# Three pieces brought together: the first stage written as one, an earlier place for the second block's residual, and another unit order in the first output product

## The reference, cut to what matters

```python
def first_block(...):
    mod = jnp.split((jax.nn.silu(c) @ w_ada[l] + b_ada[l])[:, None, :], N_MOD, axis=-1)
    ...
    h_lat = _modulate(_rmsnorm(x, norm1_g[l]), sh1, sc1)
    h_ctx = _modulate(_rmsnorm(ctx, norm1_g[l]), sh1c, sc1c)
    mix_l, mix_c = _token_mixer(h_lat, h_ctx, ...)     # begins with h @ w_in, ends with y @ w_out
    x = x + g1 * mix_l
    x = x + g2 * _swiglu(_modulate(_rmsnorm(x, norm2_g[l]), sh2, sc2), w_ffn_in[l], w_ffn_out[l])
    return _rmsnorm(x, final_norm_g)

def second_block(...):
    ...                                                # mixer: recurrence, banded attention, gates
    x = x + merged @ w_out[l]
    xn2 = rmsnorm(x, norm_ffn_g[l])
    gu = xn2 @ w_ffn_in[l]
    ff_gate, ff_up = jnp.split(gu, [D_FF_2], axis=-1)
    x = x + (jax.nn.silu(ff_gate) * ff_up) @ w_ffn_out[l]
    return rmsnorm(x, norm_final_g)
```

## Time and profile before

| what | us |
|---|---|
| median of 3 runs | 3408.72 |
| lowest, highest | 3406.57, 3416.22 |
| the profiled execution's own time | 3411.13 |
| its span | 3409.8 |
| PE busy in it | 3261.6 (96%) |
| DVE, ACT, POOL busy | 1928.6, 1379.7, 384.0 |
| mean granted TensorE clock | 0.984 |

### The profile page before, as it was taken

One profiled execution on the slowest core, in us unless ns is written; L12 is line 12 of the kernel. 1 busy time (PEld: TensorE's weight loads), 2 busy tenths in 40 slices (PEclk: granted clock), 3 DMA queues, 4 the chain that ended last, 5 costly groups with the idle time before them and its releaser, 6 DMA issues. The chain is left out here.

```text
span 3409.8 us, 39604 instructions
## 1 busy us (share of the span) xinstructions
PE 3261.6 (96%) x14862; PEld 2651.7 (78%) x14862; DVE 1928.6 (57%) x3098; ACT 1379.7 (40%) x2325; POOL 384.0 (11%) x605
## 2 busy tenths in 40 slices
PE   6999999999999999999999999998888799999998
PEld 3888888878888778888888888877556588888886
DVE  4474433456334387777445454664676587777443
ACT  4593222244333243333233355554575343333221
POOL 0121100002100300000011101111211200001011
PEclk8999999999999999999999999999999899999999
DMA  5366444346543323334852434445744523335752
GB/s 220 107 206 197 134 126 135 124 148 224 190 156 99 126 90 118 105 118 150 254 176 81 164 108 148 134 147 164 163 93 105 185 90 121 112 111 170 240 182 75
DMA packets 228045, 494.14 MB, mean 145 GB/s; under 512 B 21520, under 2 KB 84624, under 8 KB 226320
## 3 DMA queue, kind: packets, MB, share of 16 engines
q1 hardware_dynamic: 147728, 302.30, 28.0%
q0 software_dynamic: 80128, 189.30, 17.0%
HBM read 353.63 MB, written 137.89 MB: 144 GB/s over the span
## 5 line engine op out<-in xcount | busy, mean ns | idle before, releaser
L290 PE MATMUL p<-s_xh,s_wh 128*128 128x512 f32 x2256 | 901.6, 400 | 32.9 <-DVE s_tmp L401 12.3
L291 PE MATMUL p<-s_xl,s_wh 128*128 128x512 f32 x2256 | 885.3, 392 | 0.0
L292 PE MATMUL p<-s_xh,s_wl 128*128 128x512 f32 x2256 | 885.2, 392 | 0.0
L290 PEld LDWEIGHTS p<-s_xh,s_wh 128*128 128x128 f32 x2256 | 428.6, 190 | 127.3 <-issue 22.6
L292 PEld LDWEIGHTS p<-s_xh,s_wl 128*128 128x128 f32 x2256 | 427.5, 190 | 91.2
L291 PEld LDWEIGHTS p<-s_xl,s_wh 128*128 128x128 f32 x2256 | 428.4, 190 | 88.8 <-issue 1.7
L2126 PE MATMUL p<-s_xh,s_wh 128*128 128x512 f32 x1152 | 449.5, 390 | 2.1 <-DVE s_xl L2233 1.1
L2128 PE MATMUL p<-s_xh,s_wl 128*128 128x512 f32 x1152 | 448.2, 389 | 0.0
L2127 PE MATMUL p<-s_xl,s_wh 128*128 128x512 f32 x1152 | 448.2, 389 | 0.0
L250 DVE TENSOR_TENSOR s_wl<-s_ws,s_wh 128x1024 fp32r<-128x1024 f32 x157 | 195.3, 1256 | 232.9 <-ACT s_wh L242 232.6
L2126 PEld LDWEIGHTS p<-s_xh,s_wh 128*128 128x128 f32 x1152 | 216.3, 188 | 48.8 <-issue 4.2
(11 more groups left out here) (381 smaller groups left out, 5102.4 us busy)
## 6 DMA issues: line engine op xcount, KB each, us to landing
d_h<-s_fhl POOLq DMA_DIRECT2D x80, 512.0 KB, 3.2
s_ws<-i_Wf SPq DMA_DIRECT2D x48, 512.0 KB, 4.3
s_qb<-i_Wf SPq DMA_DIRECT2D x40, 512.0 KB, 4.0
s_qb<-i_Wf SPq DMA_DIRECT2D x80, 256.0 KB, 3.1
s_ws<-i_Wf SPq DMA_DIRECT2D x80, 256.0 KB, 2.9
s_aw<-i_adaT SPq DMA_DIRECT2D x32, 512.0 KB, 3.6
s_xh<-d_h POOLq DMA_DIRECT2D x16, 1024.0 KB, 12.1
s_xl<-d_h POOLq DMA_DIRECT2D x16, 1024.0 KB, 14.8
```

Of the source, the lines that this page charges most:

```text
L290: pe.matmul(o, wh, H[:, k, c:c + n], start=(k == 0), stop=False)
L291: pe.matmul(o, wh, L[:, k, c:c + n], start=False, stop=False)
L292: last = pe.matmul(o, wl, H[:, k, c:c + n], start=False, stop=(k == 7))
```

## The change

**First stage.** `stage0` now holds the context's, half 0's and half 1's work up to the first three groups. SP issues w_ada first, loads the four first weight tiles between them (two into ACC and RB, since WS has two slots), and takes x as half tiles, half 0 ahead of half 1. The weights are split while w_ada is multiplied. The squares have memory of their own; those of half 1 are made between the context's high parts and added on POOL. The spreading of half 0 stands inside the context's group, sums and spreading of half 1 inside half 0's group. The context's keys go to DRAM from ACC.

```diff
+            for k in range(8):
+                sp.dma_start(AD[:, k, :], D["ada"][k]).then_inc(*ad_in[k].up())
...
+                elif 2 <= k < 6:
+                    weights_sp(k - 1)
+                elif k == 6:
+                    x_sp(0, range(4))
+            x_sp(0, range(4, 8))
+            x_sp(1, range(8))
...
+            products_pe(firsts[0], {3: lambda: spread_pe(0)})
+            products_pe(firsts[1], {1: lambda: columns_pe(1), 3: lambda: spread_pe(1)})
+            products_pe(firsts[2])
...
+            for k in range(8):
+                high_act("c", k)
+                if k < 6:
+                    square_act(1, 2 + k)
+            for k in range(2):
+                high_act(0, k)
+            ACW.wait_ge(*w_lo.at(3))
+            for g, p in enumerate(firsts[0][1:]):
+                ACW.wait_ge(*p.mm)
+                ac.activation(ACC[:, 256 * g:256 * g + 256], B[p.bank][:, 0:256], ACT.Copy).then_inc(*evA.up())
+            al_act(0)
+            root_act(1)
+            for k in range(2, 8):
+                high_act(0, k)
```

```diff
+        pairs = plan_pairs(name, [(0, 0), (0, 1), (1, 0), (1, 1), (2, 0), (3, 0), (2, 1), (3, 1)])
...
+                products_pe(js, {5: lambda: sums_pe(s0)} if (p, h) == (2, 1) else {0: lambda: spread_pe(0, DIA[:, 0, :], s0.diag, n0.q[7])} if (p, h) == (3, 1) else None)
...
+                    norm_dve(n0, scale, shift, {1: lambda: after_dve(js), 4: lambda: weights_dve(ahead(pairs[7][2][0].i, 2))})
...
-                products_pe(e.js, {3: lambda: sums_pe(s1), 6: lambda: spread_pe(1, DIA[:, 1, :], s1.diag, q1[7])} if e is plain[0] else None)
+                products_pe(e.js, {0: lambda: sums_pe(s1), 3: lambda: spread_pe(1, DIA[:, 1, :], s1.diag, q1[7])} if e is plain[1] else None)
```

```diff
+        items += [("wo2", m, "new first", "kept", (PART[:, m, :], sc_mm.at(128)), "wo2", 1.0, TC) for m in range(4, 8)]
...
         def sp_():
+            SPW.wait_ge(*attended.scores)
+            for m in range(8):
+                residual_sp(m, 0)
+                if m < 4:
+                    for t in written[("wo2", m)]:
+                        SPW.wait_ge(*t)
+                    sp.dma_start(PART[:, m, :], dW2[m][:, 0:512]).then_inc(*part_in[m].up())
             weights_sp(ahead(pairs[0][0].i, 2) + NS)
...
+            for m in range(8):
+                SPW.wait_ge(*summed.at(m + 1))
+                residual_sp(m, 1)
...
-            products_pe(pairs[1], {6: lambda: sums_pe(s0)})
-            products_pe(pairs[2], {4: lambda: spread_pe(0, DIA[:, 0, :], s0.diag, n0.q[7])})
+            products_pe(pairs[1])
+            products_pe(pairs[2], {2: lambda: sums_pe(s0), 6: lambda: spread_pe(0, DIA[:, 0, :], s0.diag, n0.q[7])})
```

More of the change, by code:

```diff
@@ L471, in stage0 @@
         which = {"c": 0, 0: 1, 1: 2}
[L473 to L492, removed]
@@ L507, in squares_dve @@
-        def squares_dve(j):
-            what, k = sums[j]
-            if k:
-                q = slots.index(j)
-                DVW.wait_ge(*squares.at(j + 1))
-                DVW.wait_ge(*added.now())
-                dv.tensor_tensor(total[what], total[what], TMP[:, q % NT, 0:size[what]], ALU.add).then_inc(*added.up())
-        def modulated_act(what):
-            s, c, H, L, c0 = dst[what]
-            n = size[what]
-            for k in range(8):
-                q = which[what] * 8 + k
-                ACW.wait_ge(*shifted.at(q + 1))
-                ac.activation(H[:, k, c0:c0 + n], TMP[:, q % NT, 0:n], ACT.Identity, bias=shift_of[what][:, k:k + 1]).then_inc(*x_hi.up())
@@ L555, in stage0 @@
-        spread_bank = {"c": 7, 0: 4, 1: 5}
+        column_bank, spread_bank = {"c": 6, 0: 6, 1: 3}, {"c": 4, 0: 5, 1: 3}
         scale_of = {"c": GS[:, 8:16], 0: GS[:, 0:8], 1: GS[:, 0:8]}
         shift_of = {"c": MODC, 0: MOD, 1: MOD}
-        def spread_pe(what, free):
-            n = size[what]
-            PEW.wait_ge(*diag.at(which[what] + 1))
-            for t in free:
-                PEW.wait_ge(*t)
-            pe.matmul(B[spread_bank[what]][:, 0:n], ones[:], DIA[what], start=True, stop=True).then_inc(*spread.up())
@@ new lines, in ada_pe, with columns_pe @@
+        def ada_pe(k):
+            PEW.wait_ge(*silu.at(1))
+            PEW.wait_ge(*ad_in[k].at(1))
+            for c in range(4):
+                last = pe.matmul(B[c][0:2, :], sc2[:, k, :], AD[:, k, c * 512:c * 512 + 512], start=(k == 0), stop=(k == 7))
+            last.then_inc(*ada.up())
+        def columns_pe(what):
+            PEW.wait_ge(*{"c": added.at(7), 0: added.at(14), 1: added1.at(7)}[what])
+            PEW.wait_ge(*const.at(1))
+            if what == 1:
+                PEW.wait_ge(*spread3_free)
+            for j in range(size[what] // 128):
+                c = 4 * which[what] + j
+                last = pe.matmul(B[column_bank[what]][:, c:c + 1], SQ[what][0][:, 128 * j:128 * j + 128], ones[:, 0:1], start=True, stop=True)
+            last.then_inc(*colsum.up())
@@ new lines, in al_dve, with square_dve @@
+        def al_dve(part):
+            p = firsts[part][0]
+            lo = AL[32:64, p.col:p.col + p.n]
+            DVW.wait_ge(*al_hi.at(part + 1))
+            dv.tensor_tensor(lo, B[p.bank][32:64, 0:p.n], lo.bitcast(F), ALU.subtract).then_inc(*al_lo.up())
+        def square_dve(what, k):
+            n = 8 * which[what] + k
+            DVW.wait_ge(*squares.at(n + 1))
+            DVW.wait_ge(*added.now())
+            dv.tensor_tensor(SQ[what][0], SQ[what][0], SQ[what][k], ALU.add).then_inc(*added.up())
@@ L765, in pe_ @@
         def pe_():
-            for part, group in enumerate(firsts):
-                products_pe(group)
             for what, j in steps:
@@ L3328, in stage7 @@
             f = Plan()
[L3329 to L3330 removed]
+            f.m, f.done = m, summed.due()
             ready[(m, 0)] = f.done
```

598 lines of the change are left out of this document (301 added, 297 removed).

## The result

| | before | after |
|---|---|---|
| median, us (lowest to highest) | 3407.6 (3404.8 to 3416.2) | 3372.9 (3371.9 to 3373.9) |
| profiled execution, us | 3411.1 | 3372.0 |
| its span, us | 3409.8 | 3370.7 |
| PE busy, us | 3261.6 | 3253.0 |

The ratio of after to before is 0.9894, 95% interval 0.9876 to 0.9912. The change takes 34.7 us off the median. The forecast was 3365 with a range of 3352 to 3382: sign and range held. The question for the experiments is which term of the sum was too big.

What follows compares the result with a forecast made beforehand. PE, busy 3261.6 of 3409.8 us, was taken as the bound, leaving its waits and half-clock matmuls to win. Gains 22 + 3.6 + 18.4 = 44.0 off the median 3408.7 gave 3364.7, say 3365 us; range 3352 to 3382.

Steps and rivals of the forecast that it cites:

- A: First stage: half 1's group ends at 104.3 instead of 126.8 us; gain taken as 22 us, bounds 10 and 24.
- Rival 1: First stage gains only half, 11 us, because data slip or ACT or POOL is late: 3376 us; chance 0.16.
- The port beside the context's modulation: Context's group: DVE and POOL exclude each other, up to 10 us on DVE, hidden by PE's pace but for 0.5.
- B: First output product: half 1's spreading 5.0 us earlier, less 1.4 for restart, gains 3.6 us; bounds 0 and 7.
- C: Second output product: gain 19.8 us from earlier loads and covered waits, less 1.4 for restart, 18.4; bounds 12 and 20.
- Rival 2: Second output product meets a new wait, SP's weights behind eight loads or ACT's squares; C 10, 3373 us; chance 0.11.
- The cover that goes: Both blocks, at P1: less PE work follows half 1's spreading, so PE waits 8.2 and 6.9 us; restart costs 1.9.
- Rival 3: P1 does not wait because DVE's list up to it shortens: 3347 us; chance 0.06.
- Rival 4: Granted clock stays low after the two new idles at P1, making it slower, 3425 us with 60 per block; chance 0.02.
- Rival 5: The change does not do what it says, loads and sums fall where they fell: 3409 us; chance 0.03.

Runs made afterwards that it cites:

- a_only: The kernel before with only the first stage of the change, everything else old; 3387.6 us, ratio 0.9941 to before.
- weights_before_x: The change, but in the second output product SP issues the fourth pair's weights between the fourth and fifth of eight x loads; 3367.5 us.
- best: The change plus weights between x loads, half 1's spreading in first plain pair, its root before weights, last residual inside first output product's norm; 3352.2 us.
- two_raw_slots: The change, but the first stage's third and fourth weights use the two ordinary raw slots, not ACC and RB; 3378.0 us.
- b_undone: The a_and_c kernel a second time, in more rounds and beside the change; 3371.0 us, ratio 0.9888 to before.
- a_and_c: The kernel before with the change's first stage, second output product and, in the second block only, new place of half 1's sums and spreading; 3375.0 us.

## Why the prediction was right, and where it was too large

- **A, 22 forecast: right.** The landmark gives 21.7, a_only 20.8. w_ada's first product was put at 6.5 and came at 6.42, the first product at 44.5 and came at 44.59, the end of half 1's group at 104.3 and came near 105.2. The data did not slip: the slices of its trace between 5 and 46 us show 381 to 437 GB/s. Rival 1 is out.
- **The port beside the context's modulation.** A low part took 0.48 us with no POOL addition beside it (44.01) and 1.10 to 1.36 with one (46.71, 48.13, in the timelines of DVE and POOL):

```profile
44.01 0.48 DVE L695 SCALAR_TENSOR_TENSOR s_cl<-s_tmp,s_modc,s_ch 128x256 fp32r<-128x256 f32 x1 [0.18 <-ACT s_ch L622]
44.57 2.97 POOL L760 TENSOR_TENSOR s_ad<-s_ad 128x512 f32<-128x512 f32 x2 [1.75 <-ACT s_ad L610]
...
46.71 1.10 DVE L695 SCALAR_TENSOR_TENSOR s_cl<-s_tmp,s_modc,s_ch 128x256 fp32r<-128x256 f32 x1
```

PE waited 0.47 us for one of them, which is the 0.5 that was taken off. By the Trainium skill (SBUF — State Buffer, Who interferes with whom) of two such operations the later one waits until the other is done; the trace agrees, in so far as the low part begun at 46.71 ended at 47.81, behind POOL's addition, which ended at 47.54.
- **B, 3.6 forecast, 1.4 by the means of the first stretch: its steps right, its worth not.** Against the profile of before P1 came 4.8 us earlier relative to the mark (427.5 against 432.3 us) and the restart behind it cost 1.5, as forecast, 5.0 and 1.4. But the base was one trace. Three other executions with the old order took 2 to 4 us less than that one up to L2168, and the medians show no gain. What failed is the step that takes 1201.66 of the earlier trace rows as the place of the old spreading: counted from the mark it stands at 393.5 us there, at 390.6 to 391.5 in the other three. Some 2 to 3 of the 5.0 us were the bad luck of the one execution. The granted clock accounts for 1.6 of them. From half 0's sums to half 1's spreading before took 26.1 us and the other three 24.4 to 24.5, and of these four only before has a stretch at half clock within 8 us behind the sums. Windows of PE (us, busy, granted clock, DMA share, GB/s) behind the sums in before, then in a_only:

```profile
1175.60:1183.60 8.00, 8.00 (x32) 0.79 0.09 33
```

```profile
1149.20:1157.20 8.00, 7.46 (x34) 1.00 0.09 33
```

In before PE had waited 1.33 us for POOL there, in the others at most 0.96. Whether the longer wait brought the half clock was not tested.
- **C, 18.4 forecast, 12.9 measured (516.5 to 503.6 with the two traces of the change): the mis-sized term.** The step that failed is "issued at 2669, landed 2673, split by 2677; wanted at 2684". On after's time, with the end of the second pair (2644.8 there, 2671.4 in the prediction) as the common point, these are 2642.4, 2646.4, 2650.4 and 2657.7. Measured were issue at 2646.26, the first weight at 2653.39 and both split by 2657.45: 7 us late, and just in time for PE's fourth pair. Half of that came from the third pair's weights, which were put at split by 2664.1 (2637.5) and were split by 2641.65; DVE's additions, and behind them SP, waited for these. The other half is the transfer, 7.1 us and not 4, behind loads of x; put ahead of the last four of these loads, in weights_before_x, it took 4.0. And the weights had been asked only when PE would need them. They were wanted first by the lists of ACT and DVE, in which they stand ahead of half 0's root. weights_before_x gives 5.4 of the missing 5.5 us back.
- **Rival 2** ("SP's weights behind the eight loads", C of 10) named the mechanism, put at 0.11. It came true for some two thirds of its size, 5.5 of 8.4 us less in C, with a wait of 4.74 us. The measured 3372.9 lies outside the 3358 to 3371 that the prediction gave to its own sum; the stated range held because it took this rival in.
- **P1.** The cover that goes was forecast right: 8.2 and 6.9 us of waiting, 8.16 and 6.88 measured, and a granted clock of 0.56 in the 5 us behind the second (2728 to 2733), 1.00 from 2733. Rivals 3, 4 and 5 are out: P1 waits, no low stretch lasts, and the lists do what they say. One figure was wrong without effect: PE's own work from the old place of the spreading to P1 was put at 34 us, where two k-steps and three pairs at the same prices are 35.4.
- **The sum.** 21.7 + 1.4 + 12.9 = 36.0 against 34.7 of the medians; forecast 44.0. Of the 8.0 us between the two sums, 5.5 are C, 2.2 are B and 0.3 is A; the last 1.3, between 36.0 and the medians, are within the scatter.

## What to carry to other kernels

When a transfer is late, ask who stands next behind it in the list of each engine that touches it, not only when its final consumer needs it: here weights that were just in time for PE cost 4.7 us of waiting, because the engines' lists put something urgent behind them. And price a transfer by what is issued just ahead of it: 7.7 us to landing behind loads of x, 4.0 ahead of them. Move a step in steps of known size to learn whether the thing behind it is bound to it (4.1 us later here cost 4.0 and 4.1 us), before the length of a wait is counted as gain. And take the base of a term that is smaller than 5 us from several executions, or from the same stretch in several kernels.

## What the runs showed that I had not expected

**The same idle does not always bring the half clock.** After 3.08 us of idle at 108 us the granted clock was 0.50 for 3 to 6 us in most executions (2.9 us in best, 6.1 in the change), and stayed at 1.00 in others. The idle is the same in all of them, and up to there all but two_raw_slots do the same work. Windows of PE (us, busy, granted clock, DMA share, GB/s) of the change, then of b_undone:

```profile
108.20:110.00 1.80, 1.70 (x8) 0.50 0.42 105
110.00:112.00 2.00, 2.00 (x11) 0.50 0.88 295
```

```profile
108.20:110.00 1.80, 1.80 (x17) 1.00 0.62 146
110.00:112.00 2.00, 2.00 (x15) 1.00 0.76 303
```

From there to the next wait, at 175 or 172 us, the change took 66.7 us and b_undone 63.9: 2.8 us by chance. The full clock stayed in two of thirteen traces (b_undone and a_and_c, the same kernel, whose part up to there is that of the others); in two_raw_slots it fell only 1.5 us after PE had gone on.

**Stretches that the change does not touch vary by several us between executions.** From the first matmul behind half 1's group to the mark before the first output product they take 671.7 to 678.7 us, in the attention stage (from the wait of 6.8 us near 2280 to its last one) 327.2 to 334.3. That is more than the worth of B, and it explains why the stretches in the table agree with each other better than the medians do.
